# A 31-tap depthwise convolution shared out anew among TensorE, VectorE and GpSimd

## The reference, cut to what matters

```
def conformer_conv(u, dw_w, dw_b, ln_g, ln_b):
    a, gate = jnp.split(u, 2, axis=-1)
    h = a * jax.nn.sigmoid(gate)
    h = lax.conv_general_dilated(
        h, dw_w[:, None, :], window_strides=(1,),
        padding=[(CONV_WIDTH - 1, 0)],
        dimension_numbers=('NWC', 'WIO', 'NWC'),
        feature_group_count=MIX_WIDTH) + dw_b
    h = layer_norm(h, ln_g, ln_b)
    return jax.nn.silu(h)

u = jnp.dot(x, conv_w_in[j])
y_mix = conformer_conv(u[..., :2 * MIX_WIDTH], ...)
q_mem = u[..., 2 * MIX_WIDTH:]
y_mem = memory_attention(q_mem.reshape(b_, s_, MEM_HEADS, HEAD_DIM), mem_k, mem_v)
y = jnp.dot(jnp.concatenate([y_mix, y_mem], axis=-1), w_o[i])
x = layer_norm(DEEPNORM_ALPHA * x + y, ln1_g[i], ln1_b[i])
f = hierarchical_moe(x, w_rg[i], b_rg[i], w_re[i], b_re[i], w_gate[i], w_up[i], w_down[i])
```

## Time and profile before

| what | value |
|---|---|
| time, median of 3 runs | 2197.72 us (2197.64 to 2198.76) |
| span of the profiled execution | 2195.8 us |
| granted TensorE clock, mean | 0.985 |
| PE busy / DVE busy / ACT busy / POOL busy | 2071.9 / 1123.6 / 774.0 / 62.8 us |
| input projection of the first mixer on PE | about 30 to 77 us from the start |
| taps, sums and squares on PE | 77.8 to 124.3 us |
| output projection ends on PE | about 151 us |

### The profile page before, as it was taken

The page is one execution under the profiler, slowest core; times in us unless marked ns, Lnnn a source line. Parts: engine busy times, 40 slices in busy tenths (PEclk is TensorE's granted clock), DMA queues, the critical chain, the costliest instruction groups (busy, mean ns, idle before and its releaser), DMA issues.

```text
span 2195.8 us, 28571 instructions
## 1 busy us (share of the span) xinstructions
PE 2071.9 (94%) x11872; PEld 1440.3 (66%) x11872; DVE 1123.6 (51%) x1943; ACT 774.0 (35%) x1465; POOL 62.8 (3%) x96
## 2 busy tenths in 40 slices
PE   8989999989979899999899799999999999999998
PEld 7974434334448744343343587998888888998887
DVE  5964332222265632222222667567674676667665
ACT  4751111011034411101010455544554455544552
POOL 3000000000000000000000000010000000010000
PEclk9999999999989999999999899999999999999999
DMA  8628999999982689999999653454554713454552
GB/s 271 219 83 362 428 427 427 427 427 427 425 299 96 269 358 427 428 427 428 427 428 424 233 182 111 154 174 163 184 189 154 258 66 142 173 192 163 192 191 77
DMA packets 132327, 600.20 MB, mean 273 GB/s; under 512 B 6060, under 2 KB 30768, under 8 KB 105824
## 3 DMA queue, kind: packets, MB, share of 16 engines
q1 hardware_dynamic: 127888, 590.37, 67.9%
q10 hardware_dynamic: 3072, 6.74, 0.8%
q0 software_dynamic: 1232, 1.19, 0.4%
HBM read 597.22 MB, written 1.05 MB: 272 GB/s over the span
## 4 chain that ended last, share of the span: by engine, by line
PE 73%; DMA 17%; DVE 6%; ACT 3%; SPq 1%; issue 1%; DVEq 0%; ACTq 0%
PE ps L1717 12%; DMA ring<-in_w_up 10%; PE ps L485 7%; PE ps L1761 7%; PE ps L471 6%; PE ps L473 6%; PE ps L472 6%; DMA rx<-in_w_up 5%; PE ps L484 3%; PE ps L615 2%; PE ps L1010 2%; PE ps L1646 2%; PE ps L1647 1%; PE ps L3146 1%; PE ps L3148 1%; PE ps L3147 1%
## 5 line engine op out<-in xcount | busy, mean ns | idle before, releaser
L447 DVE TENSOR_TENSOR CL<-ring,CH 128x1024 fp32r<-128x1024 f32 x284 | 333.3, 1214 | 201.9 <-ACT CH L442 200.4
L1717 PE MATMUL ps<-ring,ARM 128*64 128x512 f32 x1024 | 349.1, 602 | 26.1 <-DMA ring<-in_w_up 20.2
L1717 PE MATMUL ps<-rx,ARM 128*64 128x512 f32 x1024 | 349.8, 602 | 24.5 <-DMA rx<-in_w_up 16.5
L442 ACT ACTIVATE CH<-ring 128x1024 fp32r<-128x1024 f32 x284 | 283.5, 1046 | 125.1 <-PE ps L3148 57.3
L1735 DVE TENSOR_TENSOR ARM<-ARM,ps 128x512 f32<-128x512 f32 x32 | 22.0, 687 | 438.7 <-PE ps L1717 438.7
L485 PE MATMUL ps<-XTHL,CH 128*128 128x512 f32 x704 | 240.6, 396 | 0.0
L1717 PEld LDWEIGHTS ps<-rx,ARM 128*64 128x64 f32 x1024 | 111.3, 139 | 183.0 <-issue 143.6
L1717 PEld LDWEIGHTS ps<-ring,ARM 128*64 128x64 f32 x1024 | 112.0, 139 | 175.7 <-issue 135.3
L471 PE MATMUL ps<-XTHL,CH 128*128 128x256 f32 x752 | 219.5, 292 | 0.5 <-ACT AB L1536 0.5
L473 PE MATMUL ps<-XTHL,CL 128*128 128x256 f32 x752 | 212.7, 283 | 0.0
L472 PE MATMUL ps<-XTHL,CH 128*128 128x256 f32 x752 | 212.6, 283 | 0.0
(11 more groups left out here) (456 smaller groups left out, 3757.5 us busy)
## 6 DMA issues: line engine op xcount, KB each, us to landing
rx<-in_w_gate SPq DMA_DIRECT2D x34, 2048.0 KB, 24.4
ring<-in_w_up SPq DMA_DIRECT2D x32, 2048.0 KB, 27.1
ring<-in_w_gate SPq DMA_DIRECT2D x30, 2048.0 KB, 25.4
ring<-in_w_down SPq DMA_DIRECT2D x30, 2048.0 KB, 26.6
ring<-in_w_ffn SPq DMA_DIRECT2D x30, 2048.0 KB, 8.2
rx<-in_w_up SPq DMA_DIRECT2D x28, 2048.0 KB, 27.2
rx<-in_w_down SPq DMA_DIRECT2D x26, 2048.0 KB, 27.1
ring<-in_w_in SPq DMA_DIRECT2D x14, 2048.0 KB, 9.0
```

What stands on the lines that cost most here:

```text
L442: a.e.activation(pc.hi[:, cs], pc.ap[:, cs], ACT.Copy).then_inc(act_done, a.put("hi", pc.k, q))
L447: v.e.tensor_tensor(pc.lo[:, cs], pc.ap[:, cs], pc.hi[:, cs].bitcast(F), ALU.subtract).then_inc(dve_done, v.put("lo", pc.k, q))
L1717: i = p.e.matmul(b[64 * x:64 * x + 64, :], m.XG[:, c, s0 + 64 * x:s0 + 64 * x + 64], us[x].ap[:, c, :], start=c == 0, stop=c == 7)
```

## The change

GpSimd makes all 31 taps of block 2, as a product into one of three buffers and an addition (61 instructions: 31 tensor_scalar, 30 tensor_tensor, each waiting for all but its last one), after `pool_angles` and after DVE's `hp 2`. PE keeps 10 of block 3's taps in place of 22 (72 in all). DVE has blocks 0 and 1 and 21 of block 3: 20 in the loop, 55 in `taps_b`, 8 in `taps_c`, and these 8 wait for the instruction just before them. The router's preparation is split: layer 0 after `taps_b`, layer 1 after the centring of block 3. Both maxima stand at step 3; the exponentials of the first pair stand ahead of a half piece of weights, those of the second behind it, and the other half piece comes after the first sigmoid. `dve_lam(0)` goes from step 8 to 9. ACT's square of block 1 and DVE's centring of block 2 wait for GpSimd's last tap.

```
-            for l in range(2):
-                w = WR[:, 288 * l:288 * l + 288].rearrange("p (c n) -> p c n", c=8)
...
+            v.wait_ge(route_in, ROUTE_IN)
+            v.wait_ge(pe_done, p.at("t", conv_jobs[1].tag, 1))
...
-        ON_PE = 22
+        ON_PE = 10
-        taps_b = [(k, j) for i in range(21) for k, j in ((10 + i, 0), (10 + i, 1), (i, 2))]
-        taps_c = [x for i in range(10) for x in ((21 + i, 2), (ON_PE + i, 3)) if x[0] < 31]
+        taps_b = [x for i in range(21) for x in ((10 + i, 0), (10 + i, 1), (ON_PE + i - 8, 3)) if x[0] >= ON_PE]
+        taps_c = [(k, 3) for k in range(23, 31)]
+        PRODUCTS = [mix_area(0, k, 256) for k in (10752, 6580, 9140)]
...
             for s, n in enumerate(U_ORDER):
-                if s % 2 == 0:
+                if s == 4:
+                    a_exp(conv_jobs[0])
+                    a_next("mix0", 4, 1)
+                    a_exp(conv_jobs[1])
+                elif s == 5:
+                    a_next("mix0", 4)
+                elif s % 2 == 0:
                     a_next("mix0", 2 + s // 2)
-                if s == 4:
-                    for job in conv_jobs:
-                        a_exp(job)
...
                 a.wait_ge(dve_done, v.at("c", j))
+                if n == 1:
+                    a.wait_ge(pool_done, g.at("conv", 2))
...
-                if s % 2 == 0:
+                if s in (4, 5):
+                    v_next("mix0", 4, s - 3)
+                elif s % 2 == 0:
                     v_next("mix0", 2 + s // 2)
-                if s in (3, 4):
-                    v_max(conv_jobs[s - 3])
+                if s == 3:
+                    for job in conv_jobs:
+                        v_max(job)
...
-                if s == 2:
-                    dve_router()
-                if s == 8:
+                if s == 9:
                     dve_lam(0)
...
             dve_lam(1)
+            dve_router(0)
+            for k, j in taps_c[0:4]:
+                tap(k, j, 0)
+            v.wait_ge(pe_done, p.at("first mean"))
+            v.e.tensor_scalar(M0, tile("first mean")[:, 0:256], 1.0 / 256, None,
+                              ALU.mult).then_inc(dve_done, v.put("first mean"))
+            for k, j in taps_c[4:6]:
+                tap(k, j, 0)
+            v.own(1)
+            v.e.tensor_tensor(HC[:, 0:2, :], HC[:, 0:2, :], bc_mid(M0, 2),
+                              ALU.subtract).then_inc(dve_done, v.put("c", 0))
+            v.name("c", 1)
+            tap(*taps_c[6])
+            centred(4, tile("conv", 4)[:, 0:256], p.at("conv", 4))
+            v.name("conv", 4)
+            tap(*taps_c[7])
+            v.wait_ge(pool_done, g.at("conv", 2))
             v.e.tensor_tensor(HC[:, 2, :], HC[:, 2, :], M0, ALU.subtract).then_inc(dve_done, v.put("c", 2))
+            v.own()
             centred(3, HC[:, 3, :], 0)
+            dve_router(1)
...
+        def pool_conv():
+
+            j, made = 2, []
+            g.wait_ge(dve_done, v.at("hp", j))
+            for k in range(31):
+                w, x = DWJ[:, j, k:k + 1], HP[:, j, k:k + 256]
+                if k == 0:
+                    g.e.tensor_scalar(HC[:, j, :], x, w, VT[:, j:j + 1], ALU.mult, ALU.add).then_inc(pool_done, g.put())
+                    continue
+                g.own(1)
+                g.e.tensor_scalar(PRODUCTS[k % 3], x, w, None, ALU.mult).then_inc(pool_done, g.put())
+                if k > 1:
+                    g.own(1)
+                    g.e.tensor_tensor(HC[:, j, :], HC[:, j, :], PRODUCTS[(k - 1) % 3], ALU.add).then_inc(pool_done, g.put())
+            g.own()
+            g.e.tensor_tensor(HC[:, j, :], HC[:, j, :], PRODUCTS[0], ALU.add).then_inc(pool_done, g.put("conv", j))
```

More of the change, by code:

```diff
@@ L890, in dve_memory, with dve_router @@
             v.e.tensor_copy(DW, tile("vec", 1)[:, 0:186]).then_inc(dve_done, v.put("vec", 1))
-        def dve_router():
-            b = mix_area(0, 6836, 288).rearrange("p (c n) -> p c n", c=8)
+        def dve_router(l):
+            b = mix_area(0, 288 * l, 288).rearrange("p (c n) -> p c n", c=8)
             v.wait_ge(route_in, ROUTE_IN)
-            for l in range(2):
-                w = WR[:, 288 * l:288 * l + 288].rearrange("p (c n) -> p c n", c=8)
[L899 to L906, removed]
+            v.wait_ge(pe_done, p.at("t", conv_jobs[1].tag, 1))
+            w = WR[:, 288 * l:288 * l + 288].rearrange("p (c n) -> p c n", c=8)
+            v.own()
+            v.e.tensor_tensor(b, w, bc_end(GF[:, l, 1, :], 36), ALU.mult).then_inc(dve_done, v.put())
+            v.own()
+            v.e.tensor_tensor(w, w, bc_end(GF[:, l, 0, :], 36), ALU.mult).then_inc(dve_done, v.put("router", l))
+            v.e.reduce_sum(RB[:, l, 1, :], b.rearrange("p c n -> p n c"), AX.X).then_inc(dve_done, v.put())
+            v.own()
+            v.e.reduce_sum(RB[:, l, 0, :], w.rearrange("p c n -> p n c"),
+                           AX.X).then_inc(dve_done, v.put("router parts"))
         def dve_router_sums():
@@ L1079, in dve_conv, with tap @@
         def dve_conv():
-            def tap(k, j):
+            def tap(k, j, others=1):
                 w = DWJ[:, j, k:k + 1]
@@ L1091, in tap @@
                 else:
-                    v.own(1)
+                    v.own(others)
                     v.e.scalar_tensor_tensor(HC[:, j, :], HP[:, j, k:k + 256], w, HC[:, j, :], ALU.mult,
@@ L1127, in dve_conv @@
             dve_lam(1)
[L1128 to L1141, removed]
+            dve_router(0)
[15 more added lines that the diff above has]
+            v.wait_ge(pool_done, g.at("conv", 2))
+            v.e.tensor_tensor(HC[:, 2, :], HC[:, 2, :], M0, ALU.subtract).then_inc(dve_done, v.put("c", 2))
             v.own()
-            v.e.tensor_tensor(HC[:, 2, :], HC[:, 2, :], M0, ALU.subtract).then_inc(dve_done, v.put("c", 2))
             centred(3, HC[:, 3, :], 0)
+            dve_router(1)
             for job in conv_jobs:
```

1 line of the change is left out of this document (added).

## The result

| | before | after |
|---|---|---|
| median of 4 runs each, alternating | 2198.2 us | 2210.77 us (2209.65 to 2211.18) |
| span of the profiled execution | 2195.8 us | 2207.8 us |
| granted TensorE clock, mean | 0.985 | 0.979 |

The ratio is 1.0059, with a 95% interval of 1.0047 to 1.007: slower by some 12.6 us, against 11 forecast.

A forecast was written before the change was run, and what follows sets the result against it. PE's 84 taps were taken to bound the first mixer; 8.6 us gained without blocking, but about 20 lost to it, moved the stage's end from 124.3 to 135.5, plus 11: 2208.5 us, range 2198 to 2220.

The forecast's parts named there:

- The loop's gain: Projection loop: PE's stall at step 6 and the slow matmuls behind it go, 1.8 + 1.6 = 3.4 us.
- The undisturbed sum: First mixer without blocking: conv 1 ends at 100.2, a tail of 15.3 ends the stage at 115.5, -8.6 us.
- The blocking (A): DVE's taps beside GpSimd: they exclude each other, about 20 us lost, PE waits some 17; 2206 to 2217, chance 0.62.
- GpSimd's product: Block 2's tensor_scalar on GpSimd: nearer to a memset than to the addition, costing DVE 0.2 us each, bounds 0.13 and 0.49.
- The waits added: ACT's square of block 1 and DVE's centring of block 2: GpSimd done by 114 against 127, so they cost nothing.
- The sum: End of the first mixer's squares: 120 + 15.3 = 135.5 against 124.3, plus 11 us.
- Rival C: DVE's taps starve GpSimd: two pass per GpSimd instruction, GpSimd ends at about 127, plus 9, 2207 us; chance 0.06.
- D: GpSimd's tensor_scalar slow by itself, 1.2 us or more, making GpSimd the bound: plus 13, at 1.6 plus 26; chance 0.06.
- B: DVE's `taps_b`: no blocking, every tap at 0.397 beside GpSimd, both engines end level, 2189.1 us; chance 0.17.
- The clock: PE behind its wait for blocks 0 and 1: a lower clock for some us costs 1.7, still within DVE's 15.3.

The follow-up runs named there:

- e1_loop_only: Kernel before with only the projection loop's new order of maxima, exponentials, weights and router, no GpSimd taps: 2194.88 us, ratio 0.998.
- e2_no_pool_taps: Changed kernel with GpSimd making only one of block 2's 31 taps, the other thirty left out: 2190.47 us, ratio 0.9961.
- e5_tt_products: Changed kernel with GpSimd's products as two-input tensor_tensor, the weight broadcast, in place of tensor_scalar: 2216.01 us, ratio 1.0083.
- e3b_write_only: Changed kernel with thirty GpSimd taps replaced by 211 memsets of the product buffers, which read nothing from SBUF: 2204.25 us.
- e4_nobody_waits: Changed kernel with block 2's sum and square made of another buffer, GpSimd awaited only at the normalisation: 2205.96 us, ratio 1.0026.
- e6_ten_taps: Kernel of e1_loop_only with block 2's first ten taps on GpSimd and ten fewer on DVE: 2196.72 us, ratio 0.9998.

## Why the prediction came out right, and where its steps were wrong

**The loop's gain (3.4 us): right.** It is 3.6 at the first tap, counted from K; e1_loop_only alone brought 3.4 at the squares.

**The undisturbed sum (T = 100.2, end 115.5): right within 1.0.** e2_no_pool_taps, set to the K of the kernel before, had 101.1 and 116.5. The tail of 15.3 behind T was 15.4 there and 15.4 in e5_tt_products.

**The blocking (A): the mechanism is shown, its size was off.** e2_no_pool_taps shows that GpSimd's instructions bring the taps to 0.62 us, and e3b_write_only that writing alone doesn't. The Trainium skill (SBUF — State Buffer, section Who interferes with whom) gives it as a lock between VectorE with two SBUF inputs and a GpSimd instruction that reads SBUF. This case agrees: 0.398 a tap beside 211 memsets, 0.62 beside instructions that read. DVE's loss to a product and an addition together was forecast as 0.2 + 0.49 = 0.69 us, the second term from the lone pairs of the earlier trace rows. Measured it is 1.87 - 3 x 0.397 = 0.68, and the three taps from 106.38 on bear out both terms, 0.22 and 0.47. Wrong was the time that product and addition take together: 1.46 (61 instructions at a mean of 0.73) in the prediction, 1.87 measured, because the product starts 1.07 before its addition and takes 0.92 by itself. By T some 23 of the 30 products with their additions were through, and 23 x 0.68 is 16 us, less what fell beside DVE's instructions on PSUM. Measured from K, the changed kernel's T is 13.9 later than e2_no_pool_taps's (93.4 and 79.5), where the forecast had all 30 before T and 20 us. With the K of the kernel before, T would be 115.0 and not 120. Hence also PE's wait of 12.4 and not 17, and GpSimd's end at 129.5 and not at about 114.

**GpSimd's product: mis-sized.** Its bounds came from a memset (0.21) and the addition (about 0.6 of reading), and the true value lies above both. For the lower bound the prediction named the Trainium skill (GPSIMD Engine Reference, section Engine selection: one-input work at roughly line-rate). This case speaks against that: the one-input product took 0.92 alone where the two-input addition took 0.72, and VectorE's own one-input tensor_scalar of this shape, with two operations, takes 0.41 (82.60 in the trace before). As a two-input instruction the same product of GpSimd passed in 0.75 (93.26 to 94.01 in e5_tt_products).

**"The waits added: nothing": wrong by 3 to 4 us.** They rested on GpSimd's end at 114. It was 129.5, DVE waited 3.90 and ACT 5.1, and with the waits gone the stage ended 3.2 earlier (e4_nobody_waits).

**The sum: right, by errors that largely cancel.** The forecast of the squares' end was 100.2 + 20 + 15.3 = 135.5. Counted with the K of the kernel before, the runs have 101.1 + 13.9 + 18.9 = 133.9 (18.9 is the tail with 3.9 of waiting in it): 6 too much for the blocking, nearly 4 too little for the wait, and 1 too little for the undisturbed T. This execution's late K adds 0.8. Rival C had said why the first two should cancel: the order of who waits changes little, since the sum of both engines' claims stays the same. That is an argument which fits these figures; no run tested it by itself. The time itself, 2208.5, is 0.2 below its own terms (2195.8 + 11 + 1.9 = 2208.7). The measured case lies between A and C: 1.5 taps passed for each of GpSimd's instructions, where A had about one and C two. C's end for GpSimd, 127, is nearer than A's 114, and "a POOL that ends after 125 would mean C or D" came true. With 0.06 on C, the chance was on the wrong side of the two. D is half true: the product was slow by itself, but below the 1.2 us from which it was to decide. B fell at the taps' 0.62, against 0.397.

**The clock.** PE's mean and five taps behind its wait took 2.08 and 3.20 us where e1_loop_only's took 1.03 and 2.32: 1.9 us, against 1.7 in the sum. It was hidden, since DVE and GpSimd were later.

**What stays open.** The squares and SP's load moved by 10.3 us, the span by 12.0, and the second block's first load of `in_w_in` by 11.7 (1196.28 to 1208.00). So some 1.4 us came in between, in the experts of the first block. No run looked for them, and they need not be the change's: in the two profiles of e1_loop_only's kernel the way from the squares' end to the end of the span differs by 3.1 (2071.9 and 2075.0). Why K itself varies, from 20.1 to 22.4, is open too.

## What to carry to other kernels

Before work is given to GpSimd beside a VectorE stream with both inputs in SBUF, price it as an exchange: what GpSimd's instructions take from the stream, per unit of work. Here a tap on GpSimd cost VectorE 0.68 us beside its taps and would have cost it 0.397 to make itself, so moving taps brought VectorE no time, even where nobody waited (e6_ten_taps: 5.2 to 5.6 us for ten taps worth 4.0), and a faster GpSimd made it worse (e5_tt_products). And a wait costed at nothing is only as good as the estimate of when the other engine ends: carry both ends of that estimate to the wait. When two profiles are compared, count from an event that the change leaves alone: here K moved by up to 2.2 us, as much as some of the effects.

## What the runs showed of the hardware that was not expected

- A GpSimd tensor_scalar of 128x256 with a weight for each partition is slower than its tensor_tensor of the same shape: 0.92 against 0.72 us alone, and 1.07 against 0.81 from start to start beside VectorE's taps.
- The exclusion is not a strict alternation for it: three taps pass by a product and an addition, two by two tensor_tensors. Two of the three start within the product and one within the addition.
- GpSimd's memsets (210 in 53.3 us) didn't slow VectorE's taps at all: 14.34 us for 36, as without them.
- The exclusion works both ways: a product of GpSimd took 2.95 us beside two splits of weights of 128x1024, which took 2.88 themselves in place of 2.35.
